# Feed-forward block in groups of three, four and four, with seven-product tiles from the fourth block on

## The reference

```python
n2 = _rms(h, norm_ffn_w[l])
up = _causal_dwconv(n2 @ w_up[l], ffn_dw_w[l], ffn_dw_b[l])   # w_up: 1024 x 5632, 3 taps
gate, val = jnp.split(up, 2, axis=-1)                         # 2816 gates, 2816 values
h = h + (jax.nn.silu(gate) * val) @ w_down[l]                 # w_down: 2816 x 1024
```

## Time and profile before

| | us |
|---|---|
| median of 3 runs | 1810.31 (1810.08 to 1810.60) |
| the profiled execution, its own time | 1810.64 |
| its span in the profile | 1808.8 |
| PE busy in the span | 1791.1 |
| DVE busy in the span | 1398.2 |
| ACT busy in the span | 965.0 |

### The profile page before, as it was taken

One profiled execution on the slowest core, in us unless ns is written; L12 is line 12 of the kernel. 1 busy time (PEld: TensorE's weight loads), 2 busy tenths in 40 slices (PEclk: granted clock), 3 DMA queues, 4 the chain that ended last, 5 costly groups with the idle time before them and its releaser, 6 DMA issues.

```text
span 1808.8 us, 32729 instructions
## 1 busy us (share of the span) xinstructions
PE 1791.1 (99%) x13630; PEld 1707.8 (94%) x13630; DVE 1398.2 (77%) x2450; ACT 965.0 (53%) x1884; POOL 159.4 (9%) x134
## 2 busy tenths in 40 slices
PE   9999999999999999999999999999999999999998
PEld 8999999978899989899899999999899999999987
DVE  5888897678756788968889797979358888787844
ACT  6223332568734446536566565657347566666632
POOL 0000000000000002011011212120000112121000
PEclk9999999999999999999999999999999999999999
DMA  6222222200132247565357777775332677767431
GB/s 197 94 79 85 94 94 71 94 24 25 64 107 76 77 130 161 135 151 127 105 129 152 158 157 153 158 154 127 117 94 77 134 161 151 161 149 159 117 119 70
DMA packets 248610, 211.90 MB, mean 117 GB/s; under 512 B 6550, under 2 KB 244943, under 8 KB 248462
## 3 DMA queue, kind: packets, MB, share of 16 engines
q1 hardware_dynamic: 184030, 177.81, 31.6%
q0 software_dynamic: 64416, 31.99, 14.4%
q10 hardware_dynamic: 16, 0.00, 0.0%
HBM read 207.69 MB, written 2.10 MB: 116 GB/s over the span
## 4 chain that ended last, share of the span: by engine, by line
PE 90%; DVE 5%; ACT 3%; DMA 1%; issue 0%; SPq 0%; DVEq 0%
PE ps L659 42%; PE ps L700 31%; PE ps L1300 5%; PE ps L1352 5%; DVE wlo L2337 1%; PE ps L888 1%; PE ps L1141 1%; PE ps L1119 1%; ACT p L1614 1%; PE ps L1132 1%; PE ps L1144 1%; PE ps L913 1%; DVE ast L2621 0%; PE ps L1153 0%; PE ps L1123 0%
## 5 line engine op out<-in xcount | busy, mean ns | idle before, releaser
L2337 DVE TENSOR_TENSOR wlo<-raw,whi 128x1024 fp32r<-128x1024 f32 (+1 forms) x361 | 436.8, 1214 | 196.0 <-ACT whi L1386 194.7
L1386 ACT ACTIVATE whi<-raw 128x1024 fp32r<-128x1024 f32 (+1 forms) x361 | 378.5, 1050 | 242.6 <-PE ps L659 115.2
L659 PE MATMUL ps<-nhi,whi 128*128 128x264 f32 (+3 forms) x1456 | 329.2, 290 | 2.6 <-DVE clo L2605 0.8
L659 PE MATMUL ps<-nhi,wlo 128*128 128x264 f32 (+3 forms) x1456 | 325.0, 288 | 0.0
L659 PE MATMUL ps<-nlo,whi 128*128 128x264 f32 (+3 forms) x1328 | 287.9, 287 | 0.0
L659 PEld LDWEIGHTS ps<-nhi,whi 128*128 128x128 f32 x1456 | 236.8, 189 | 6.6 <-DVE clo L2605 1.0
L659 PEld LDWEIGHTS ps<-nhi,wlo 128*128 128x128 f32 x1456 | 236.0, 189 | 2.1
L700 PE MATMUL ps<-thi,whi 128*128 128x256 f32 x784 | 224.9, 287 | 1.2 <-DVE wlo L2337 0.5
L700 PE MATMUL ps<-thi,wlo 128*128 128x256 f32 x784 | 221.6, 283 | 0.0
L700 PE MATMUL ps<-tlo,whi 128*128 128x256 f32 x784 | 221.4, 282 | 0.0
L659 PEld LDWEIGHTS ps<-nlo,whi 128*128 128x128 f32 x1328 | 211.5, 189 | 1.9
(11 more groups left out here) (474 smaller groups left out, 3591.5 us busy)
## 6 DMA issues: line engine op xcount, KB each, us to landing
raw<-in_w_in_dram SPq DMA_DIRECT2D x90, 1024.0 KB, 5.8
raw<-in_w_up_dram SPq DMA_DIRECT2D x22, 1024.0 KB, 5.1
raw<-in_w_out_dram SPq DMA_DIRECT2D x20, 1024.0 KB, 4.9
s1t<-in_w_in_dram SPq DMA_DIRECT2D x49, 256.0 KB, 3.3
s1t<-in_w_in_dram POOLq DMA_DIRECT2D x49, 256.0 KB, 6.6
raw<-in_w_in_dram POOLq DMA_DIRECT2D x49, 256.0 KB, 4.7
raw<-in_w_down_dram SPq DMA_DIRECT2D x16, 512.0 KB, 3.4
raw<-in_w_conv_out_dram SPq DMA_DIRECT2D x4, 1024.0 KB, 4.9
```

The lines of the kernel that those rows point to most:

```text
L659: mm = eng.matmul(o, w, m[:, k, a:b], start=begins, stop=final and n == len(ks) - 1 and i == 2)
L1386: eng.activation(hi, raw, ACT.Copy).then_inc(*A.up("hi", s))
L2337: eng.tensor_tensor(lo, raw, hi.bitcast(F), ALU.subtract).then_inc(*V.up("lo", s))
```

## The change

The groups become three, four and four blocks instead of four, four and three, and all gates and values from block 3 on go by seven. Before, gates of blocks 4 to 10 and values of blocks 5, 6, 7, 8 and 10 did. The two numbers in SP's program are the slot numbers at which two small loads (`FAR`, `PBC`) are issued, written from the end of the list now; with eight more slots in the list they stand at the same places.

```diff
         SEVEN = [(0, KT, 0, 128, 0), (0, 4, 0, 128, 1), (0, 4, 0, 256, 2), (4, 8, 0, 256, 3)]
         SEVEN_AT = [0, 4, 1, 2]
-        GROUPS = [(0, 4), (4, 8), (8, 11)]
+        GROUPS = [(0, 3), (3, 7), (7, 11)]
         DOWN = [(0, 0), (1, 0), (0, 1), (1, 1), (2, 0), (2, 1), (3, 0), (3, 1)]
-        GATES_BY_SEVEN, VALUES_BY_SEVEN = range(4, 11), (5, 6, 7, 8, 10)
+        GATES_BY_SEVEN, VALUES_BY_SEVEN = range(3, 11), range(3, 11)
...
-                elif s == 159:
+                elif s == len(slots) - 263:
                     on.wait_ge(V("al", 2 * NFF - 1), T("up_all", 2))
                     eng.dma_start(FAR, decay).then_inc(*FAR_IN.up("in"))
-                elif s == 408:
+                elif s == len(slots) - 14:
                     on.wait_ge(T("mixed_all"))
```

## The result

The changed kernel takes 1818.14 us (median of 7 runs, 1815.44 to 1821.77), the kernel before 1810.31 in the same series (7 runs, 1808.80 to 1811.77). The ratio is 1.0043 (95% interval 1.0033 to 1.0052): slower by 0.43%, and beyond the upper end of the predicted range. The profiled execution, the shortest of the seven, took 1815.44 us with a span of 1813.6, 4.8 us more than that of before.

A forecast was written before the change was run, and what follows sets the result against it. PE, busy 1791.1 of 1808.8 us, was taken as the bound. 1810.64 - 5.44 + 0.56 + 4.0 + 0.46 + 1.93 = 1812.15, less 0.33 for the median: 1811.8, no change forecast; range 1807.0 to 1816.0.

The forecast's parts named there:

- four waits: The sum's added waits of PE: 0.56 us at d5, 4.0 for slot 2, 0.46 and 1.93 at two group ends.
- The saving: Four units in blocks 3, 4 and 9 go from column to seven, saving 1.36 us each, 5.44 in all.
- d5: First group's shortened `w_down`: PE waits 0.56 us for DVE's split of d5.
- Slot 2: Block 3's gates: PE waits 4.0 us, two products in, for DVE's late split of slot 2.
- DVE's 0.48 us per unit: Runs of units by seven: DVE takes 10.56 us per unit against PE's 10.08; no wait counted inside the group.
- The step that failed: Eight more accumulating DMAs of POOL and four loads of `s1t` in the long stretches: counted as nothing.
- its 0.96 us of room: Second group's last unit: slot 2's split ends 0.96 us before its use; half remains after 0.48 more lateness.
- The clock falls in the wait: Rival: during slot 2's 4.0 us wait PE's clock falls, costing 3 us more: 1814.8, slower; chance 0.15.
- The row at the span's end: PE idle from 1802.50; clock still 1.00 up to 1805.80, 0.50 from 1806.00; slot 2's wait is about that long.
- The group ends: Start of `w_down`: PE waits 1.93 us for `21` behind ACT's wait for d1's load; 0.46 more in second group, 1.93 in third.
- the 5.00 of the sum: Group ends: the load of d1, for which ACT stands waiting, taken at 5.00 us.

The follow-up runs named there:

- thin: Changed kernel, POOL's two accumulating transfers per `w_up` unit cut to a quarter of their rows; 1813.25 us, 1.0014 against the kernel before.
- order_thin: As thin, with DVE making token sums 0 and 1 first and slot 2's split before the last pieces of `rescale`; 1808.92 us, 0.9997.
- old_groups: Changed kernel with groups of four, four and three as before, all units of blocks 4 to 10 by seven; 1810.14 us, 1.0002.
- col3: Changed kernel with its new groups, but block 3 by column; 1816.58 us, 1.0036 against the kernel before.
- thin_raw: Changed kernel with only POOL's accumulating transfer into `raw` cut to a quarter of its rows; 1814.66 us, 1.0027 against the kernel before.
- tail2: Changed kernel with `prep` left out at two calls in a group's last unit, so ACT does `21` before the copy of d1; 1810.52 us, 1.0009.
- again: The changed kernel once more, unedited; 1817.45 us, 1.0036 against the kernel before.
- tail: Changed kernel with one call of `prep` left out; ACT's order came out unchanged, so a third series of it; 1815.96 us, 1.0032.

## Why the prediction was wrong

Its forecast was no change, as the sum of a gain and four waits of about the same size. These came as forecast, and two things came on top, one taken at nothing and one held for a rival.

- **The saving**: right. The units by seven take 10.08 us where nothing waits, as in the kernel before.
- **d5**: 0.4 us lost against 0.56 forecast.
- **Slot 2**: right in place, size and cause. PE lost 3.9 us against 4.0; thin showed that an earlier load doesn't help, order_thin that an earlier place in DVE's order does.
- **DVE's 0.48 us per unit**: right as a period (10.57 against 10.56), and of no consequence inside the groups, as forecast.
- **The step that failed** is "Four more units mean eight more accumulating DMAs of POOL and four loads of `s1t`, at a DMA share of 0.71 in the long stretch; I count nothing for them". In the third group the loads of `w_up` come to 8.1 to 9.5 us, where the longest of the kernel before is 7.6. A raw buffer is filled every second unit, 20.16 us; in the chain of the first profile 9.50 for the load, 5.72 for the sum and 1.07 for the copy are 16.3 of them, and the splits must still follow. What doesn't fit makes ACT late, and ACT's order makes PE wait: 0.9 to 2.8 us in the third group's units of three profiles. Thinning the sums into `s1t` brings the loads down to 6.0 at the most, and thinning both kinds takes 2.7 us off the median on the same chip; old_groups shows a loss of the same kind with eight units in one group alone. The prediction looked inside the groups for DVE's split of slot 2 and its 0.96 us of room, not for an ACT copy.
- **The clock falls in the wait** was a rival at 0.15, and it happened. Of the nine profiles of kernels with slot 2 waited for 2.0 us or more and nothing put in the gap, all show 0.94 to 0.97 from 600 to 660; in those with filling, with a wait of 1.5 or without a wait there it is 1.00, and col3, which waits 3.4 us there for its banks, has 0.94. The price was 1.6 us in the first profile and, from the stretches of thin_raw, 4.00 x 0.50 + 4.00 x 0.23 = 2.9 in another; the prediction took 3 for the rival and nothing in the sum, and named this fall as a sign that it is wrong. The row at the span's end was the right one to look at; what was weighed wrong is a wait "hardly longer than that idle": a wait of 2.0 was enough. The rule of the Trainium skill, "TensorE: Matmul & The Clock Gate", Part 1: The HAM clock gate, that an idle PE is put to half clock, agrees with these rows. Waits are not all that the clock falls after: in the profile of the kernel before it is 0.58 and 0.56 in the two stretches from 372 to 376 us, and no listed wait from 360 to 380 is over 0.8. The rows of the prediction leave this out; its matmuls at 1.2 GHz could have been read for the price.
- **The group ends**: the mechanism was right (tail2 took both waits away by letting `21` go first), a size was off. The second lost 1.7, 1.2 and 2.5 us in three profiles against 1.93 forecast; the third 1.1, 3.7 and 2.5, also against 1.93, and the clock fell there in one of the three. ACT stands there for the load of d1, which took 4.4 to 5.6 us in these six places against the 5.00 of the sum. So that load varies and hasn't become longer, and the third end still loses time with shorter loads of `w_up` (2.6 us of waiting in thin). In the median the two ends cost more than the 3.86 us of the sum: tail2's ratio is 0.0023 to 0.0034 below the three series, 4.2 to 6.2 us.

The three profiles of the changed kernel can be summed from here. To the forecast's 1812.15 come 1.6 for the clock in the first, -0.3 at d5 and slot 2, 0.9 inside the third group, -0.2 and -0.8 at the ends: 1813.4; as its feed-forward part began 2.1 us later than before, 1815.5 against 1815.44 measured. For again it is 1812.15 + 1.6 - 0.3 + 1.6 - 0.7 + 1.7 + 1.9 = 1818.0 against 1817.91, and for tail, which began 1.1 earlier, 1812.15 + 1.7 - 0.3 + 2.8 + 0.5 + 0.6 - 1.1 = 1816.4 against 1816.21. So these terms hold the miss of the three profiled executions, about a us of it, on average, from before the part that was changed. The execution at the first series' median, 1818.14, has no profile. What stays open is why the loads, and with them the terms inside the group and at the ends, vary so much between executions of one program.

## What to carry to other kernels

Before lengthening a run of units that reload in a fixed rhythm, add up the whole loop of one buffer (load, what is added to it, copy, splits) at the transfer times of the busiest stretch and with the added transfers as company; the mean DMA share doesn't show that it is full. Look which instruction of an in-order engine stands for the transfer, and what is queued behind it: letting the one that PE waits for go first was a small edit here, and brought the ratio from 1.0032 or more to 1.0009. And count a wait of PE of 2 us or more with the clock that it may cost afterwards.

## What was not expected of the hardware

- A wait of 2.0 to 3.7 us in the middle of dense work halved PE's clock for some 3 to 6 us behind it; waits of that size at a group's end did so in some executions (2.6 us in thin) and not in others (2.3 in tail).
- A product of 128x128 float32 ones takes 0.22 us (30 in 6.6), nearly twice the 0.12 of one matmul by seven with 258 tokens, so that 16 of them fill 3.7 us. The trace shows each as two matmuls (x32 for 16).
- Loads of 1 MB beside accumulating transfers of 256 KB took 8.1 to 9.5 us in the third group, and 5.2 to 6.0 where the transfers into `s1t` were cut to a quarter, though the mean DMA share only rises from 0.71 in the kernel before's long stretch to 0.77 in the third group.
- The beginning of the feed-forward part differs between executions of one program by about 3 us (538.05 to 541.26 for the changed kernel), in part with the clock of the first 25 us (0.93 and 0.86).
